# Solve stage of a hybrid token mixer: chunk masks and exponentials ahead of the low-rank decays, block and solution buffers in pairs

## The chip, the cores and the metric

The kernel runs on one core of one Trainium2 chip. The metric is the device time of one execution in microseconds; three executions of the kernel before are given, and one more was profiled.

## The reference

One layer of a bidirectional mixer over 1024 latent tokens and 256 context tokens, width 1024, all float32. The projected tokens feed two head groups. The first is gated DeltaNet (four heads, key and value width 128), computed in chunks. What the kernel calls the solve belongs to it:

```
diff = gc[..., :, None] - gc[..., None, :]
decay = where(incl, exp(where(incl, diff, 0)), 0)
lower = where(strict, einsum("nbhcd,nbhsd->nbhcs", kb, k) * decay, 0)
sol = triangular_solve(eye + lower, rhs, lower=True, unit_diagonal=True)
attn = einsum("nbhcd,nbhsd->nbhcs", q, k) * decay
```

The second is gated linear attention (GLA: four heads, key width 64, value width 128). It needs its own projections of q, k and v, and a decay per channel from a low-rank product:

```
gk = log_sigmoid(einsum("blzr,zrc->zblc", lr, w_gk) + b_gk) / 16
```

Both scan forward and backward. An output projection, a gated residual and a convolutional feed-forward network follow.

## The kernel before

The program is a sequence of blocks. In a block each of five engines (PE for matmuls, ACT for activations, DVE for vector work, POOL for vector work and memsets, SP for issuing DMAs) walks through its own list, written out by hand; semaphores order them, and the engines meet at a block's end. The change lies in the second block, the **solve stage** (lines 753 to 1167 in the trace). The first block makes the normalised inputs `hT`, the DeltaNet q, k, v and the product `lrab`; the block behind it scans the DeltaNet chunks.

The tokens are ten chunks of 128, taken in the order of `ORDER`; index m below is the place in that order, and d is the direction, forward or backward. The stage does three kinds of work side by side.

**The units** are GLA projections on PE, evacuated by ACT from three PSUM banks in turn (`unit`, L833 to L857 on PE; `evac`, L931 to L953 on ACT). A unit is 512 tokens wide, or 256 for the third part of a tile. `V0` to `V3` are value tiles (L851), `Q0`, `Q1`, `K0`, `K1` query and key tiles (L855), and `D0` to `D3` the low-rank decay products (L843, only 32 rows deep). The list `UNITS` numbers them; unit n waits for the evacuation of unit n-3 (L839). After a tile's last evacuation ACT issues the load of the weights two tiles on into `ws` (L953).

**The chunks**: `keys(m)` on PE makes the products k k and, for latent chunks (m from 2), k q (L871, L877). SP loads the cumulated decays of a chunk as rows broadcast to all partitions into `GR`, three buffers in turn (`g_rows`, L769), a buffer's next load waiting until the chunk that used it is done. POOL adds the mask (`mask`, L1044), ACT takes eight exponentials (`decays_of`, L977), DVE multiplies the products by them into `Wm` and `Am` (`chunk`, L1088 and L1094), SP stores those (`store`, L775 and L779).

**The solves**: three batches of 4, 4 and 2 chunks. SP reads 32x32 diagonal blocks of the stored `Wm` back into `blk` (`feed`, L787). DVE scales them into `co` (L1100, L1102) and runs 31 pairs of steps (`solve`, L1109 and L1112), each pair waiting for the one before. The result is in `so`, cleared by POOL before (`clear`, L1036), transposed by POOL into `st` after (`turned`, L1050), and stored by SP (`solutions`, L793 to L797). There is one `blk` and one `so`, so the next batch's `clear` waits until the stores of the batch before have landed.

**Low-rank decays**: `decay(j)` on ACT takes Abs, Exp and Ln of the 1280 columns of a D tile (L965 to L969), `decay(j)` on DVE one elementwise pass and a scan over them (L1076, L1079). They have one scratch tile `ga`.

At the start the gate tables are made by ACT and DVE in turn (L982 to L992, L1117 to L1146) with two small groups of PE products between (L889, L895), and end in the tile `rows`, from which SP stores what `g_rows` reads. At the end PE sums the modulation (`mg`, 32 products of one column each, L926), and DVE adds it up (L1164, L1166).

```
solve(0)
for m in range(6, NT):
    chunk(m)
solve(1)
solve(2)
```

Of the kernel before, what the change touches and what calls it, by code (L numbers as in the profile page):

```python
# [22 lines left out]
H = 4  # L23
# [62 lines left out]
def program(nc, x, c, ctx, c_ctx, w_mod, b_mod, norm1, w_in, gdn_conv, gdn_a_log, gdn_dt_bias, gdn_norm,  # L86
# [9 lines left out]
    with es:  # L96
# [113 lines left out]
        wlr = place("wlr", [P, KT, 48], 83)  # L210
        s_lw = sem("w_lrab_in")
# [22 lines left out]
        with nc.Block() as block:  # L234
            @block.sync
            def _(sp):
# [53 lines left out]
                rest(15)  # L290
                sp.wait_ge(s_ma, 64)
# [4 lines left out]
                sp.wait_ge(s_lw, 32)  # L296

# [399 lines left out]
        ws = [place(f"ws{i}", [P, KT, P], 142.25 + 4 * i) for i in range(2)]  # L697
# [5 lines left out]
        blk = place("blk", [P, BLK, BLK], 184)  # L703
        co = place("co", [P, BLK, BLK], 180)
        so = place("so", [P, BLK, BLK], 176)
# [16 lines left out]
        s_gr, s_grm, s_pm = [two(f"g_rows_in{u}") for u in range(3)], two("g_rows_masked"), two("decays")  # L722
# [8 lines left out]
        mg = [place(f"mg{i}", [P, 2, 512], (150.25, 159.25, 142.25, 146.25)[i]) for i in range(4)]  # L731
# [3 lines left out]
        for name in ("D0", "V0.0", "D1", "V0.1", "V0.2", "D2", "D3", "V1", "V2", "V3", "Q0", "Q1", "K0", "K1"):  # L735
# [17 lines left out]
        with nc.Block() as block:  # L753
            @block.sync
            def _(sp):
                def weights(n):
                    sp.dma_start(ws[n % 2][:, :, :], win[:, :, WCOL[n]:WCOL[n] + P]).then_inc(s_w3[n % 2], 16)

# [22 lines left out]
                def feed(b):  # L781
# [3 lines left out]
                    if b:  # L785
                        sp.wait_ge(s_sv, STEPS_S * b)
                    sp.dma_start(blk[0:32 * n, :, :], blocks_of(w_img, 2 * m0, 2 * n)).then_inc(s_fd[b], 16)  # L787

                def solutions(b):
# [3 lines left out]
                    sp.dma_start(blocks_of(x_img, 2 * m0, n), so[f, :, :]).then_inc(s_xw[b], 16)  # L793
                    sp.dma_start(blocks_of(xt_img, 2 * m0 + n, n), so[k, :, :]).then_inc(s_xw[b], 16)
# [4 lines left out]
                weights(0)  # L799
                sp.dma_start(v_dram.rearrange("c p n -> p c n"), vtok[:, :, :]).then_inc(s_vs, 16)  # L800
                weights(1)
# [13 lines left out]
                for m in range(4, 6):  # L815
                    store(m)
                    g_rows(m + 3)
                solutions(0)
                for m in range(6, 8):
# [14 lines left out]
            def _(pe):  # L834
                def unit(n):
# [21 lines left out]
                    mm.then_inc(s_um, 1)  # L857
# [26 lines left out]
                tile("D0")  # L884
                unit(UNIT[("V", 0, 0)])
# [6 lines left out]
                tile("D1")  # L892
# [34 lines left out]
                mm.then_inc(s_mq, 1)  # L927

# [1580 lines left out]
```

## Time and profile before

| | us |
|---|---|
| median of three runs | 1782.11 |
| lowest and highest | 1780.32, 1782.6 |
| profiled execution, its own time | 1779.76 |
| its span in the trace | 1777.7 |
| solve stage, first to first instruction of the next block | 298.4 to 505.2 |
| ACT's part of the gate tables, first Abs to the end of the sigmoid | 304.6 to 309.9 |
| PE's last product in the stage ends | 488.6 |
| DVE's last solve step ends | 498.9 |

The mean granted clock of PE is 0.956 over the span, where 1.00 is 2.4 GHz and 0.50 is 1.2 GHz. In a timeline each line is a run of like instructions of one engine: when the run starts, how long it takes, and in brackets how long the engine sat idle before it and who released it. The matmul counts of the trace are twice those of the program for float32.

### The profile page before, as it was taken

What the parts mean: (1) busy time and instruction counts of PE and PEld (TensorE: products, weight loads), DVE (VectorE), ACT (ScalarE), POOL (GpSimd) and SP (SyncE); (2) the same over time, 40 slices, a digit from 0 to 9 for tenths busy, and PEclk for the clock granted to TensorE, in tenths of its full rate; (3) what the DMA queues carried; (4) which work ended last, traced back from release to release, by engine and by line L of the source; (5) the groups of instructions that cost most, each with busy time, mean ns of one, the idle gap of its engine ahead of it and who ended that gap; (6) DMA issues with size and microseconds to landing.
All of it is one profiled execution on the core that took longest, in us unless ns stands there. A gap on an engine that the chain in (4) does not pass through costs nothing.

```text
span 1777.7 us, 20877 instructions
## 1 busy us (share of the span) xinstructions
PE 1651.0 (93%) x8249; PEld 1229.4 (69%) x8249; DVE 1217.4 (68%) x1747; ACT 554.8 (31%) x890; POOL 461.1 (26%) x436
## 2 busy tenths in 40 slices
PE   7997999899949979999949989999999999999997
PEld 2544545696649965665537768888888888788786
DVE  2548876376656648888765639999999998633635
ACT  2623233561023332222243432222222222332322
POOL 4000000422013326566422343333333332300000
PEclk9998998899869988999969999999999999999999
DMA  9374454367369841000032321111111111532242
GB/s 335 97 266 130 142 179 153 98 178 190 65 189 274 231 127 60 12 25 24 15 122 89 107 71 49 48 48 48 48 48 48 48 48 48 201 95 95 90 148 83
DMA packets 202172, 194.23 MB, mean 109 GB/s; under 512 B 41045, under 2 KB 156063, under 8 KB 201948
## 3 DMA queue, kind: packets, MB, share of 16 engines
q1 hardware_dynamic: 194972, 187.40, 33.6%
q10 hardware_dynamic: 6816, 5.24, 1.0%
q8 instruction: 65, 1.06, 0.2%
q14 instruction: 31, 0.25, 0.1%
q0 software_dynamic: 288, 0.27, 0.0%
HBM read 150.77 MB, written 42.11 MB: 109 GB/s over the span
## 4 chain that ended last, share of the span: by engine, by line
PE 47%; DVE 7%; ACT 2%; DMA 2%; issue 2%; POOL 1%; SPq 0%; ACTq 0%; POOLq 0%
PE PS L2115 9%; PE PS L2117 9%; PE PS L2119 9%; PE PS L2152 4%; PE PS L2154 4%; PE PS L2156 4%; PE PS L1622 4%; PE PS L1635 2%; DVE Qbd L1833 2%; DMA ogb<-og_spill 2%; POOL xr L2312 1%; DVE AT L1849 1%; PE PS L1670 1%; DVE Ex L1814 1%; DVE oss L2344 0%
## 5 line engine op out<-in xcount | busy, mean ns | idle before, releaser
L2432 DVE SCALAR_TENSOR_TENSOR acc<-PS,fcol,acc 128x945 f32<-128x945 f32 (+2 forms) x176 | 215.2, 1222 | 35.4 <-ACT acc L2195 29.9
L2432 DVE SCALAR_TENSOR_TENSOR act<-PS,fcol,act 128x945 f32<-128x945 f32 (+2 forms) x176 | 215.1, 1222 | 21.6 <-ACT act L2195 16.2
L2115 PE MATMUL PS<-h2hi,whi 128*128 128x512 f32 x704 | 219.9, 390 | 0.0
L2117 PE MATMUL PS<-h2lo,whi 128*128 128x512 f32 x704 | 219.7, 389 | 0.0
L2119 PE MATMUL PS<-h2hi,wlo 128*128 128x512 f32 x704 | 219.5, 389 | 0.0
L384 PE MATMUL PS<-hT,wq 128*128 128x512 f32 (+1 forms) x432 | 163.1, 537 | 0.0
L2302 POOL TENSOR_TENSOR wlo<-wu,whi 128x1024 fp32r<-128x1024 f32 x44 | 106.5, 2421 | 216.7 <-ACT whi L2188 216.7
L2117 PEld LDWEIGHTS PS<-h2lo,whi 128*128 128x128 f32 x704 | 132.5, 188 | 27.5
L2119 PEld LDWEIGHTS PS<-h2hi,wlo 128*128 128x128 f32 x704 | 132.4, 188 | 27.5
L2115 PEld LDWEIGHTS PS<-h2hi,whi 128*128 128x128 f32 x704 | 132.5, 188 | 27.4
L2443 DVE TENSOR_TENSOR wrlo<-wr,wrhi 128x1024 fp32r<-128x1024 f32 x41 | 50.2, 1225 | 129.6 <-ACT wrhi L2258 129.6
L384 PEld LDWEIGHTS PS<-hT,wq 128*128 128x128 f32 x432 | 82.0, 190 | 80.0 <-issue 77.3
L1622 PE MATMUL PS<-hT,wz 128*128 128x512 f32 x256 | 119.0, 598 | 0.0
L2152 PE MATMUL PS<-wrhi,ahi 128*128 128x512 f32 x352 | 109.5, 393 | 5.1 <-DVE yb L2451 2.2
L2154 PE MATMUL PS<-wrlo,ahi 128*128 128x512 f32 x352 | 109.9, 393 | 0.0
L2156 PE MATMUL PS<-wrhi,alo 128*128 128x512 f32 x352 | 109.6, 393 | 0.0
L2258 ACT ACTIVATE wrhi<-wr 128x1024 fp32r<-128x1024 f32 x44 | 46.7, 1060 | 152.9 <-DMA wr<-in_w_down_dram 152.9
L2195 ACT ACTIVATE act<-PS,fcol 128x1024 f32<-128x1024 f32 x22 | 26.6, 1207 | 205.8 <-PE PS L2119 205.8
L2328 POOL TENSOR_TENSOR act<-act,acc 128x1024 f32<-128x1024 f32 x22 | 53.7, 2442 | 107.7 <-DVE act L2432 107.7
L2152 PEld LDWEIGHTS PS<-wrhi,ahi 128*128 128x128 f32 x352 | 66.5, 189 | 20.0 <-issue 2.6
L851 PEld LDWEIGHTS PS<-ws,hT 128*128 128x128 f32 x640 | 76.5, 202 | 2.0 <-ACT gP L937 2.0
L851 PE MATMUL PS<-ws,hT 128*128 128x128 f32 x640 | 77.2, 285 | 0.6 <-ACT gP L937 0.6
(278 smaller groups left out, 2877.6 us busy)
## 6 DMA issues: line engine op xcount, KB each, us to landing
wm<-in_w_mod_dram SPq DMA_DIRECT2D x24, 1024.0 KB, 8.0
wu<-in_w_up_dram SPq DMA_DIRECT2D x44, 512.0 KB, 3.8
wr<-in_w_down_dram SPq DMA_DIRECT2D x44, 512.0 KB, 3.4
wq<-in_w_in_dram SPq DMA_DIRECT2D x12, 512.0 KB, 7.7
gdn_x_image<-ztile SPq DMA_DIRECT2D x10, 516.0 KB, 6.6
gdn_xt_image<-ztile SPq DMA_DIRECT2D x10, 516.0 KB, 6.3
GR<-gdn_gc_rows SPq DMA_DIRECT2D x20, 256.0 KB, 4.7
gdn_w_image<-Wm SPq DMA_DIRECT2D x20, 256.0 KB, 4.4
```

What stands on the lines that cost most here:

```text
L384: mm = pe.matmul(PS[:, BANK[kind] + b, 0:n], wq[kind][:, k, :], hT[:, k, t0:t0 + n], start=(k == 0), stop=(k == KT - 1))
L851: mm = pe.matmul(PS[:, o, q * P:(q + 1) * P], hT[:, k, t0 + q * P:t0 + (q + 1) * P], ws[wt % 2][:, k, :], start=(k == 0), stop=(k == KT - 1))
L1622: mm = pe.matmul(PS[:, 3, :], ws4[n % 2][:, k, :], hT[:, k, half * 512:(half + 1) * 512], start=(k == 0), stop=(k == KT - 1))
L2115: pe.matmul(PS[:, b + half, :], whi[k][u][:, kk, :], h2hi[:, 4 * half:4 * half + 4, kk, :], start=(kk == 0), stop=False)
L2117: pe.matmul(PS[:, b + half, :], whi[k][u][:, kk, :], h2lo[:, 4 * half:4 * half + 4, kk, :], start=False, stop=False)
L2119: mm = pe.matmul(PS[:, b + half, :], wlo[k][u][:, kk, :], h2hi[:, 4 * half:4 * half + 4, kk, :], start=False, stop=(kk == KT - 1))
L2152: pe.matmul(PS[:, 2 * t + half, :], ahi[u][:, tok], wrhi[u][:, cols], start=(f == 0), stop=False)
L2154: pe.matmul(PS[:, 2 * t + half, :], ahi[u][:, tok], wrlo[u][:, cols], start=False, stop=False)
L2156: mm = pe.matmul(PS[:, 2 * t + half, :], alo[u][:, tok], wrhi[u][:, cols], start=False, stop=(f == FT - 1))
L2302: g.tensor_tensor(wlo[k][f % 2][:, :, :], wu[k][f % 2][:, :, :], whi[k][f % 2][:, :, :], ALU.subtract).then_inc(s_wl[k], 1)
L2328: g.tensor_tensor(act[f][:, :], act[f][:, :], acc[f % 2][:, :], ALU.mult).then_inc(s_6g, 1)
L2432: tp = v.scalar_tensor_tensor(out=t_[:, r0:r1, c0:c1], in0=up[:, r0 + dr:r1 + dr, c0 + dc:c1 + dc], scalar=tap_col(j, k, f), in1=t_[:, r0: ...
```

## The change

The mathematics is unchanged. What changes is the order of the lists of all engines in the solve stage, and some buffers.

- The first value tile's weights get a buffer `wg0` that the first block already fills, from SP, behind its last weight loads. In the solve stage V0 is PE's first unit. It is split: three quarters of its first unit, the gate products, the last quarter.
- `UNITS` starts with V0, V1.0 and V1.1; the tiles D0 and D1 come behind V1.1, D2 and D3 behind V1.2 and two keys.
- DVE masks chunks 0 to 3, POOL chunks 4 to 9.
- ACT takes the exponentials of chunks 0 to 7 before any D unit, and the four low-rank decays between V2 and Q1.
- DVE works through chunks 0 to 5, and in `solve` it does other work after 13 of the 31 pairs of steps: chunks 6 and 7 in batch 0, `decay(1)` in batch 1, `decay(3)` in batch 2.
- `blk` and `so` become two buffers each, used in turn. `so1` shares its place with the second half of `gq`, so the evacuation of Q1.0 waits for all stores of batch 1. `blk1` and `st` lie over `lrab`, so their first use waits for D3.
- The loads of `mg` are issued together by ACT, and PE's `mg` products come ahead of tile K1.

The diff, cut to its core:

```diff
@@ first block, SP @@
                 rest(15)
+                sp.wait_ge(s_qu, H)
+                sp.dma_start(wg0[:, :, :], win[:, :, GV0:GV0 + P]).then_inc(s_wg0, 16)
...
@@ solve stage @@
-        for name in ("D0", "V0.0", "D1", "V0.1", "V0.2", "D2", "D3", "V1", "V2", ...
+        for name in ("V0", "V1.0", "V1.1", "D0", "D1", "V1.2", "D2", "D3", "V2", ...
...
@@ SP @@
-                    if b:
-                        sp.wait_ge(s_sv, STEPS_S * b)
+                    if b == 1:
+                        sp.wait_ge(s_um, UNIT[("D", 3, 2)] + 1)
+                    if b == 2:
+                        sp.wait_ge(s_sv, STEPS_S)
...
                 feed(1)
+                solutions(0)
                 for m in range(8, NT):
                     store(m)
+                feed(2)
                 solutions(1)
-                feed(2)
                 solutions(2)
...
@@ ACT @@
+                        if (j, b) == (1, 0):
+                            a.wait_ge(s_xw[1], 64)
                         ev = a.activation(gq[:, j, t0:t0 + w], ...
...
@@ POOL @@
                 clear(0)
+                clear(1)
                 g.wait_ge(s_mn, 1)
-                for m in range(8):
+                for m in range(4, NT):
                     mask(m)
                 turned(0)
-                clear(1)
...
@@ DVE @@
+                        if j == 12:
+                            for op, m in between:
+                                op(m)
...
+                for m in range(3):
+                    mask(m)
+                for m in range(3):
+                    chunk(m)
+                mask(3)
+                for m in range(3, 6):
+                    chunk(m)
+                solve(0, ((chunk, 6), (chunk, 7)))
+                chunk(8)
+                chunk(9)
                 decay(0)
-                chunk(0)
...
+                solve(1, ((decay, 1),))
                 decay(2)
...
+                solve(2, ((decay, 3),))
```

How the instructions stand is shown at three places. In these rows `gvtok` is the evacuation of a V unit, `gP` that of a D unit, `GR` the exponentials of a chunk (one row for each direction), `ga` a low-rank decay.

ACT before, from the second low-rank decay (`decay(1)`) to the first unit of V1:

```order
L965 ACTIVATE ga<-gP 128x1280
L967 ACTIVATE ga<-ga 128x1280
L969 ACT_TABLE_LOAD
L969 ACTIVATE ga<-ga 128x1280
L937 ACTIVATE gP<-PS,vcol 128x512 x2
L937 ACTIVATE gP<-PS,vcol 128x256
L977 ACT_TABLE_LOAD
L977 ACTIVATE GR_1461<-GR_1461,ngc 128x128 x4
L977 ACTIVATE GR_1462<-GR_1462,ngc 128x128 x4
L937 ACTIVATE gP<-PS,vcol 128x512 x2
L937 ACTIVATE gP<-PS,vcol 128x256
L941 ACTIVATE gvtok<-PS 128x4x128
```

The exponentials of one chunk (chunk 1) stand between the D tiles, and a low-rank decay ahead of them.

ACT in the change, from the evacuation of V1.0 (first row) to that of V1.2:

```order
L943 ACTIVATE gvtok<-PS 128x4x128
L981 ACTIVATE GR_1466<-GR_1466,ngc 128x128 x4
L981 ACTIVATE GR_1467<-GR_1467,ngc 128x128 x4
L981 ACTIVATE GR_1462<-GR_1462,ngc 128x128 x4
L981 ACTIVATE GR_1463<-GR_1463,ngc 128x128 x4
L981 ACTIVATE GR_1464<-GR_1464,ngc 128x128 x4
L981 ACTIVATE GR_1465<-GR_1465,ngc 128x128 x4
L943 ACTIVATE gvtok<-PS 128x4x128
L939 ACTIVATE gP<-PS,vcol 128x512 x2
L939 ACTIVATE gP<-PS,vcol 128x256
L939 ACTIVATE gP<-PS,vcol 128x512 x2
L939 ACTIVATE gP<-PS,vcol 128x256
```

The exponentials of chunks 5, 6 and 7 now stand between the evacuations of V1.0 and V1.1, and the D units behind them, with no low-rank decay near.

PE before, at the end of the stage (K0, K1, then the `mg` products):

```order
L855 MATMUL PS<-hT,ws_1456 128x512 x16
L855 MATMUL PS<-hT,ws_1456 128x256 x8
L855 MATMUL PS<-hT,ws_1457 128x512 x16
L855 MATMUL PS<-hT,ws_1457 128x256 x8
L926 MATMUL PS<-ones,mg_1482 128x1 x8
L926 MATMUL PS<-ones,mg_1483 128x1 x8
L926 MATMUL PS<-ones,mg_1484 128x1 x8
L926 MATMUL PS<-ones,mg_1485 128x1 x8
```

The one-column products close PE's list.

PE in the change, same place (K0, the `mg` products, K1):

```order
L856 MATMUL PS<-hT,wg_106 128x512 x16
L856 MATMUL PS<-hT,wg_106 128x256 x8
L927 MATMUL PS<-ones,mg_1487 128x1 x8
L927 MATMUL PS<-ones,mg_1488 128x1 x8
L927 MATMUL PS<-ones,mg_1489 128x1 x8
L927 MATMUL PS<-ones,mg_1490 128x1 x8
L856 MATMUL PS<-hT,ws_1460 128x512 x16
L856 MATMUL PS<-hT,ws_1460 128x256 x8
```

The one-column products moved ahead of the 24 products of tile K1.

DVE in the change, inside the first solve, after 13 pairs of steps:

```order
L1119 TENSOR_TENSOR blk_1479<-co,so_1482 128x19x13
L1122 TENSOR_TENSOR so_1482<-so_1482,blk_1479 128x19x13
L1092 TENSOR_TENSOR Wm_1468<-PS,GR_1462 128x512
L1092 TENSOR_TENSOR Wm_1469<-PS,GR_1463 128x512
L1098 TENSOR_TENSOR Am_1472<-PS,GR_1462 128x512
L1098 TENSOR_TENSOR Am_1473<-PS,GR_1463 128x512
L1092 TENSOR_TENSOR Wm_1470<-PS,GR_1464 128x512
L1092 TENSOR_TENSOR Wm_1471<-PS,GR_1465 128x512
L1098 TENSOR_TENSOR Am_1474<-PS,GR_1464 128x512
L1098 TENSOR_TENSOR Am_1475<-PS,GR_1465 128x512
L1119 TENSOR_TENSOR blk_1479<-co,so_1482 128x18x14
L1122 TENSOR_TENSOR so_1482<-so_1482,blk_1479 128x18x14
```

Chunks 6 and 7 stand there between two steps; before, they followed the solve's last step.

## Rows read from the trace of the kernel before

**Rows 1.** The page: busy time of the engines, share of the span, instructions.

```profile
PE 1651.0 (93%) x8249; PEld 1229.4 (69%) x8249; DVE 1217.4 (68%) x1747; ACT 554.8 (31%) x890; POOL 461.1 (26%) x436
```

**Rows 2.** PE, timeline of the stage: start us, us, engine line op out<-in xcount.

```profile
299.56 4.63 PE L843 MATMUL PS<-lrab,wgk 32*128 32x512 f32 x6
304.12 9.67 PE L851 MATMUL PS<-ws,hT 128*128 128x128 f32 x64
...
314.54 2.41 PE L843 MATMUL PS<-lrab,wgk 32*128 32x512 f32 x6
...
318.93 10.88 PE L851 MATMUL PS<-ws,hT 128*128 128x128 f32 x96
329.74 2.41 PE L843 MATMUL PS<-lrab,wgk 32*128 32x512 f32 x6
339.73 4.63 PE L843 MATMUL PS<-lrab,wgk 32*128 32x512 f32 x6 [7.58 <-ACT gP L937]
345.00 9.71 PE L851 MATMUL PS<-ws,hT 128*128 128x128 f32 x64 [0.65 <-ACT gP L937]
354.55 1.06 PE L871 MATMUL PS<-kT 128*128 128x128 f32 x8
...
358.12 10.88 PE L851 MATMUL PS<-ws,hT 128*128 128x128 f32 x96
...
422.16 55.14 PE L855 MATMUL PS<-hT,ws 128*128 128x512 f32 x144
477.14 11.44 PE L926 MATMUL PS<-ones,mg 128*128 128x1 f32 x64
```

**Rows 3.** Windows: busy us of PE, PEld, DVE, ACT, POOL, then granted clock, DMA, GB/s.

```profile
332.00:333.00 1.00, 0.15 (x1) 0.00 (x0) 0.01 (x1) 1.00 (x5) 1.00 (x1) 0.89 1.09 330
...
345.00:350.00 5.00, 5.00 (x24) 5.00 (x25) 0.60 (x2) 0.89 (x2) 0.49 (x1) 0.51 0.62 199
```

**Rows 4.** DVE, timeline of the stage.

```profile
317.34 0.42 DVE L1141 COPY rows<-PS 80x256 f32<-80x256 f32 x1 [2.13 <-PE PS L896]
...
344.35 1.26 DVE L1088 TENSOR_TENSOR Wm<-PS,GR 128x512 f32<-128x512 f32 x2
...
361.95 2.82 DVE L1079 TENSOR_TENSOR_SCAN gP<-cmask,gP 128x1280 f32<-128x1280 bf16 x1
...
434.32 1.22 DVE L1100 TENSOR_TENSOR co<-blk,nb 64x1024 f32<-64x1024 f32 x1 [2.46 <-DMA blk<-gdn_w_image]
...
447.04 0.42 DVE L1109 TENSOR_TENSOR blk<-co,so 128x252 f32<-128x252 f32 x1
...
460.79 0.19 DVE L1112 TENSOR_TENSOR so<-so,blk 128x31 f32<-128x31 f32 x1
472.73 1.21 DVE L1100 TENSOR_TENSOR co<-blk,nb 32x1024 f32<-32x1024 f32 x1 [11.75 <-DMA blk<-gdn_w_image]
```

**Rows 5.** POOL, timeline of the stage.

```profile
323.11 11.27 POOL L1044 TENSOR_TENSOR GR<-GR,mneg 128x512 f32<-128x512 f32 x6 [23.50 <-DMA GR<-gdn_gc_rows]
...
350.24 2.50 POOL L1044 TENSOR_TENSOR GR<-GR,mneg 128x512 f32<-128x512 f32 x2 [4.75 <-DMA GR<-gdn_gc_rows]
...
387.67 2.56 POOL L1044 TENSOR_TENSOR GR<-GR,mneg 128x512 f32<-128x512 f32 x2 [7.26 <-DMA GR<-gdn_gc_rows]
...
470.96 0.95 POOL L1036 MEMSET so<- 128x1024 f32 x1 [7.05 <-DMA gdn_x_image<-st]
```

**Rows 6.** SP, timeline of the stage.

```profile
374.88 0.37 SPq L787 DMA_DIRECT2D blk<-gdn_w_image  x1
...
382.84 1.63 SPq L769 DMA_DIRECT2D GR<-gdn_gc_rows  x2
```

**Rows 7.** ACT, timeline of the first block's end and of the stage.

```profile
296.53 0.38 ACT L531 ACTIVATE lrab<-PS 48x256 f32<-48x256 f32 x1 [4.24 <-PE PS L444]
...
388.98 2.56 ACT L977 ACTIVATE GR<-GR,ngc 128x128 f32<-128x128 f32 x8 [1.47 <-POOL GR L1044]
...
477.34 0.38 ACT L949 ACTIVATE gk<-PS 128x256 f32<-128x256 f32 x1 [2.86 <-PE PS L855]
```

More of the change, by code:

```diff
@@ L210, in program @@
         wlr = place("wlr", [P, KT, 48], 83)
+        wg0 = place("wg0", [P, KT, P], 142.25)
+        s_wg0 = sem("first_gla_value_weights_in")
         s_lw = sem("w_lrab_in")
@@ L296, in _ @@
                 sp.wait_ge(s_lw, 32)
+                sp.wait_ge(s_wg0, 16)
             @block.gpsimd
@@ L696, in program @@
         gq = place("gq", [P, 2, LAT], 197)
-        ws = [place(f"ws{i}", [P, KT, P], 142.25 + 4 * i) for i in range(2)]
+        ws = [wg0, place("ws1", [P, KT, P], 146.25)]
         ga = place("ga", [P, TOK], 150.25)
@@ L702, in program @@
         nb = [place(f"nb{b}", [P, BLK], 175.25 + 0.125 * b) for b in range(3)]
-        blk = place("blk", [P, BLK, BLK], 184)
+        blk = [place(f"blk{i}", [P, BLK, BLK], (192, 184)[i]) for i in range(2)]
         co = place("co", [P, BLK, BLK], 180)
-        so = place("so", [P, BLK, BLK], 176)
+        so = [place(f"so{i}", [P, BLK, BLK], (176, 201)[i]) for i in range(2)]
         st = place("st", [P, BLK, BLK], 188)
@@ L721, in program @@
         s_rd, s_nb = sem("rows_stored"), [sem(f"beta_blocks_in{b}") for b in range(3)]
-        s_gr, s_grm, s_pm = [two(f"g_rows_in{u}") for u in range(3)], two("g_rows_masked"), two("decays")
+        s_gr, s_grm, s_pm = [two(f"g_rows_in{u}") for u in range(3)], two("g_rows_masked_by_dve"), two("decays")
+        s_grp = two("g_rows_masked_by_pool")
         s_mn = sem("mask_ready")
@@ L814, in _ @@
                 feed(0)
[L815 to L819, printed above, removed]
+                for m in range(4, 8):
                     store(m)
@@ L883, in _ @@
                 tr.then_inc(s_lt, 1)
-                tile("D0")
-                unit(UNIT[("V", 0, 0)])
+                unit(UNIT[("V", 0, 0)], 0, 3)
                 pe.wait_ge(s_gd, 3)
@@ L891, in _ @@
                 mm.then_inc(s_gm, 1)
-                tile("D1")
+                unit(UNIT[("V", 0, 0)], 3, 4)
                 pe.wait_ge(s_gd, 4)
@@ L927, in _ @@
                 mm.then_inc(s_mq, 1)
+                tile("K1")
             @block.scalar
@@ new lines, in _ @@
+                decays_of(2)
+                evac(UNIT[("V", 0, 2)])
+                decays_of(3)
+                decays_of(4)
+                evac(UNIT[("V", 1, 0)])
+                decays_of(5)
+                decays_of(6)
+                decays_of(7)
+                evac(UNIT[("V", 1, 1)])
+                tile("D0")
+                tile("D1")
+                evac(UNIT[("V", 1, 2)])
+                decays_of(8)
+                tile("D2")
+                tile("D3")
+                decays_of(9)
@@ L1094, in chunk, with mask, solve @@
                             v.tensor_tensor(Am[u][d][:, :], PS[:, 6 + u, :], GR[m % 3][d][:, :], ALU.mult).then_inc(s_a[d], 1)
-                def solve(b):
+                def mask(m):
+                    for d in range(2):
+                        v.wait_ge(s_gr[m % 3][d], 16 * (m // 3) + 16)
+                        v.tensor_tensor(heads(GR[m % 3][d][:, :]), heads(GR[m % 3][d][:, :]),
+                                        mneg[:, d, :].unsqueeze(1).to_broadcast([P, H, P]), ALU.add).then_inc(s_grm[d], 1)
+                def solve(b, between):
                     n = 16 * BATCHES[b][1]
```

147 lines of the change are left out of this document (59 added, 88 removed).

## The prediction

> **What bounds the kernel now.** I read the page first: PE is busy for 93% of the span and DVE for 68% [rows 1], so time is to be had where PE waits. The front table then shows such a place: PE's last product of the solve stage ends at 488.6, the next block starts at 505.2, and between them stands DVE, whose last solve step ends at 498.9. The timelines say what each engine does there. On PE [rows 2] see three things: a gap of 7.58 us before D3, blocks of V products that take 9.7 us instead of 7.25, and no work after 488.6. On DVE [rows 4] see that batch 2 starts only at 472.73, after 11.75 us of idling for its blocks, because `so`, `blk` and SP's queue are shared. So before, the chain of solves sets the stage's end, with PE 16.6 us ahead of it. From 298.5 to 505.2 the stage takes 206.7 us. I ask how long each of the two engines needs in the new order; the later one sets the end.
>
> **DVE in the new order.** The changes there go together: second buffers, decays moved behind, 8 of 20 masks added. First the start. V0.0 takes D0's place, so the tile `rows` is copied when PE has done the transposes of `lrab` (1.1 us, from 298.5 to 299.56), V0.0 (9.7), the gate products and two transposes (0.8 + 0.2): at 310.3, plus 0.4 for the copy, 310.7 instead of 317.8 [rows 2, 4]. ACT's gate chain takes 5.3 us and now starts at about 301, in time for that. The first mask moves by the same 7.1 us, from 323.1 [rows 5] to 316.0. The masks on DVE have no row; the nearest is the multiplication of the same size, 0.63 us each [rows 4]. I take that; even at POOL's 1.25 us [rows 5] eight of them would cost 5 us more of an engine that turns out to have 24 to spare. Chunks 0 to 2 then finish at about 321, 323 and 325. From a finished chunk to the next mask on its buffer 4.6 us pass (345.6 to 350.24) [rows 4, 5], then 1.3 for two masks, 2.5 for eight exponentials [rows 7], 2.5 for the chunk: chunk 3 is done at 332.
>
> Chunk 6, in the middle of batch 0, needs keys(6), which PE reaches at 367.5 (below). From there: chunks 6 and 7, 5.0; the other 18 pairs of steps, 13.9 (447.04 to 461.0) [rows 4]; chunks 8 and 9, 5.0; decay(0), 1.5 + 2.8 = 4.3 [rows 4]: 395.7. Batch 1 takes 26.7 (434.32 to 461.0) [rows 4] and decay(1) 4.3: 426.7. Decay(2), batch 2 (26.2, from 472.73 to 498.9) and decay(3) bring DVE to 461.5. The stores and the block's end took 6.3 us after the last step (498.9 to 505.2): 467.8. If PE were no bound, the stage would end 37 us earlier. It is one, and this is where the expected gain goes.
>
> **PE in the new order.** PE's work is the same, product for product. From 298.5 to 488.6 are 190.1 us. Of that, 7.58 + 0.65 = 8.2 is idle [rows 2]. The clock costs the rest that can go: D0 and D3 take 4.63 instead of 2.41, 4.4 in all, and V0.0 and V1.0 take 9.67 and 9.71 where 64 products at the full clock take 10.88 x 64/96 = 7.25, 4.9 in all [rows 2]; the window from 345 to 350 shows the granted clock at 0.51, 1.2 GHz, to its end [rows 3]. What is left is **172.6 us**, the `mg` products' 11.4 at their present, mostly half clock included. To this the new order adds, in order of time:
>
> - V0.0 opens at half clock, as now, **2.4**. D0 was only beside it.
> - A stall at the third unit of D0, **7.3**, and it is the new wait. That unit reuses the bank of V1.1 and waits for ACT's evacuation, and ACT must first take the exponentials of chunks 5, 6 and 7. PE is there after 1.1 + 9.7 + 0.8 + 2.0 (to 318.93) + 10.9 + 3.6 + 7.25 + 3.6 + 7.25 + 1.9 = 48.1 us, at 346.6, with 3.6 for the keys of two chunks (354.55 to 358.12) [rows 2]. ACT: the rows of chunk 7 are loaded by SP behind `feed(0)`, which waits for chunk 3's stores, about 4.6 after 332, so 336.6. From that feed to the mask of the row tile queued behind it 12.8 us pass today (374.88 to 387.67) [rows 5, 6]: 349.4. Masks and exponentials end 3.9 after the mask's start (387.67 to 391.5) [rows 5, 7], the evacuation takes 0.6: 353.9. Lower bound: only SP's issues of four stores (2) and the load's own 4.8 (382.84 to 387.67) count, giving 347.9 and a stall of 1.3. Upper: every round of chunks a microsecond later, 11. I take the row that has the same feed in front.
> - After that stall the clock has fallen, as it had 0.7 us after D2 (window 332 to 333 at 0.89, then 0.50) [rows 2, 3]. The last D0 unit and D1 pay 2.22 x 1.2 = **2.7**, the V and key products behind them **2.4** like V1.0.
> - D2 and D3 in a row, 4.8 us of products 32 rows deep. D1 alone, between full products, kept the clock (2.41), but D2 with 0.7 us of idling lost it, and D3 at half clock did not bring it back: it rose only 4.9 us into V1.0 [rows 2, 3]. Between nothing and 1.8 + 2.4 = 4.2, I take half, **2.1**.
> - K1 behind the one-column products, which run at half clock (11.44 us for 64) [rows 2]: **2.4** again. Before, nothing followed them.
>
> A page speaks on the fourth item. The Trainium skill, TensorE: Matmul & The Clock Gate, Part 1, has the gate follow how busy PE is ("activity releases the throttle") and names no row count. By that, D2 and D3 would keep the clock, and the sum would be 2.1 lower; D3's row, busy from start to end and still at half clock, speaks against it.
>
> Sum: 172.6 + 2.4 + 7.3 + 2.7 + 2.4 + 2.1 + 2.4 = 191.9; PE ends at 490.4. The last evacuation takes 0.4 [rows 7]. Between the first block's last evacuation (296.9) and the next block 1.5 us passed [rows 7], semaphore clearing included, which is missing here; I take 0.7, between 0.2 and 1.5. The stage ends at **491.5 instead of 505.2: 13.7 us less**.
>
> **Edits costed at nothing.** The load of `wg0` stands in the first block behind SP's last weight load and lands while PE still has q, k, v and `lrab` products to do; without that cover V0.0 would start later by a load's 4 us or so. Batch 1's wait for D3 lies under chunks 8 and 9. The `mg` loads go out after V3, some 40 us before PE needs them. The evacuation of Q1.0 waits for batch 1's stores: DVE 426.7 plus 10.0 (460.98 to 470.96) [rows 4, 5] is 436.7. PE has that product at 490.4 - 19.6 - 11.4 - 17.2 - 6.9 = 435.3 (an eighth of 55.14 is a unit, 6.9 [rows 2]) and needs the bank only two units later, at 449.1. So 12.4 us cover it.
>
> The next block begins with loads from DRAM as before; I expect nothing there. In the profiled execution the time goes from 1779.76 to 1766.1. The median lies 2.35 above that execution, so I forecast 1782.1 - 13.7 = **1768.4** for a median.
>
> **Rivals.**
> 1. *PE is released early*: the loads behind `feed(0)` come without queueing, the stall is 1.3 and the D tiles keep the clock. 172.6 + 2.4 + 2.4 + 1.3 = 178.7, 13.2 below my sum: 1755.2. For it: D1's row. Against: 7.26 us of POOL waiting for row tiles even now [rows 5]. Chance 0.15; half ways to it lie in my range.
> 2. *Chunks run late*: keys(2) needs the first chunk's `Wm`, and PE gets there at 323.0, one or two us after it. If the first six row loads and masks take 5 us more, PE waits there 3.5 and at D0 3.5 more: 1775.4. For it: POOL's six masks took 11.27 instead of 7.5 [rows 5]. Chance 0.17.
> 3. *Slower*: the store of batch 1 comes so late that Q1.0's bank is not free. Every us beyond 12.4 is paid by PE; from 12.4 + 13.7 = 26.1 us on the kernel is no faster than before, and at 35 it takes 1782.1 + 8.9 = 1791. DVE would need a wait of that length ahead of batch 1, for instance decay(0) waiting for ACT behind V2.0. ACT has that at about 389, DVE asks at 391. Chance 0.03.
> 4. *The solves still bound the stage*: the moved work in the middle of each batch brings waits of 20 us, DVE and PE end together or DVE ends last, near 498: 1775 to 1782. Chance 0.05.
>
> **How the numbers follow.** My case, 1763 to 1773, has 0.60. The range 1758 to 1777 takes in rival 2 and part of 1 and 4. Both bounds of the stall (6.0 down, 3.7 up) with the clock's 2.1 either way give 8 down and 6 up around 1768.4, which the range holds. What a measurement here can tell from no change is 0.2%, 3.6 us. Rivals 1 and 2 and my case are all faster: 0.94 with most of rival 4; same 0.03, slower 0.03.
>
> **What would show it.** PE's last product of the stage is one of K1, ends near 490, and DVE has by then been done for over 20 us. PE has one idle gap of 5 to 10 us in D0, ended by the evacuation of V1.1, behind ACT waiting for POOL's mask of chunk 7. K1 takes about 19.6 us, V0.0's 64 products about 9.7. Wrong would be: DVE or SP last in the stage; a wait of ACT at Q1.0 that PE feels; a first block that ends later than 298.4; or a gap at keys(2).

## The result and the profile after

The changed kernel takes **1762.43 us** (median of four runs, 1760.85 to 1766.8); the kernel before took 1782.36 beside it (four runs, 1780.32 to 1782.66). The ratio on record is 0.9905, with a 95% interval of 0.9885 to 0.9925: faster by 0.95%. The quotient of the two medians alone is 0.9888; the kernel before had medians of 1780.2 to 1780.3 in the later series below, so a gain of 17 to 20 us is what the runs bear out. The forecast was 1768.4 with a range of 1758 to 1777. The profiled execution took 1761.43 us, 18.3 less than the 1779.76 of the profiled execution before; its span in the trace is 1759.5.

The page of the changed kernel, first part, answers to [rows 1]:

```profile
PE 1645.4 (94%) x8249; PEld 1224.1 (70%) x8249; DVE 1223.1 (70%) x1755; ACT 555.5 (32%) x890; POOL 441.9 (25%) x428
```

The instructions of PE are the same in number; it is busy for 5.6 us less in all, so most of the gain is time in which it stood. DVE has eight instructions more (the masks) and POOL eight fewer.

PE's timeline of the stage after the change, against [rows 2] (`...` stands for lines left out):

```profile
299.53 0.80 PE L884 MATMUL PS<-ident,lrab 48*128 48x48 f32 x10 [1.98 <-PEq L107]
300.25 7.20 PE L852 MATMUL PS<-wg,hT 128*128 128x128 f32 x48
...
308.11 2.03 PE L852 MATMUL PS<-wg,hT 128*128 128x128 f32 x16
...
344.26 1.98 PE L844 MATMUL PS<-lrab,wgk 32*128 32x512 f32 x4
354.85 5.48 PE L844 MATMUL PS<-lrab,wgk 32*128 32x256 f32 x8 [8.61 <-ACT gvtok L943]
360.26 6.10 PE L852 MATMUL PS<-ws,hT 128*128 128x128 f32 x32
...
369.87 4.56 PE L844 MATMUL PS<-lrab,wgk 32*128 32x512 f32 x12
374.35 7.41 PE L852 MATMUL PS<-wg,hT 128*128 128x128 f32 x64
...
458.42 8.54 PE L927 MATMUL PS<-ones,mg 128*128 128x1 f32 x64
466.82 19.43 PE L856 MATMUL PS<-hT,ws 128*128 128x512 f32 x48
486.97 1.06 PE L1339 MATMUL PS<-ident,kT 128*128 128x128 f32 x8 [0.72 <-PEq L759]
```

PE works to the very end: its last K1 product ends at 486.25 and the next block follows 0.7 us later, where before 16.6 us lay between. One stall is left, the 8.61 us at the third unit of D0, and it is the one that was forecast, with the releaser that was forecast: the evacuation of V1.1.

DVE's timeline after, against [rows 4]: a wait for keys(6), the start of batches 1 and 2, the end of the last solve.

```profile
367.29 1.29 DVE L1092 TENSOR_TENSOR Wm<-PS,GR 128x512 f32<-128x512 f32 x2 [5.99 <-PE PS L873]
...
396.89 1.19 DVE L1110 TENSOR_TENSOR co<-blk,nb 64x1024 f32<-64x1024 f32 x1
...
434.43 1.19 DVE L1110 TENSOR_TENSOR co<-blk,nb 32x1024 f32<-32x1024 f32 x1
...
464.44 0.18 DVE L1122 TENSOR_TENSOR so<-so,blk 64x31 f32<-64x31 f32 x1
```

The idle times in front of `co` (2.46 and 11.75 us before) are gone, and DVE is done with the solves at 464.6 instead of 498.9, 22 us ahead of the stage's end. The two engines have changed places. The stage takes 187.4 us from PE's first product to that of the next block (299.53 to 486.97), where it took 206.7. The rest of the program is as before: 1272.6 us from the stage's end to the end of the span (486.93 to 1759.5), and 1272.5 before (505.2 to 1777.7).

The wait behind the solves does come, as the prediction had it: ACT waits for batch 1's stores ahead of Q1.0, and PE does not feel it. ACT's timeline after:

```profile
437.84 0.60 ACT L948 ACTIVATE gq<-PS 128x512 f32<-128x512 f32 x1 [2.21 <-DMA gdn_x_image<-st]
```

### The profile page after: what moved, and what is told of

Read it like the earlier page. It is cut to its first block, busy times and chain, and to the rows that moved or that the text cites. A ratio compares the mean times of both kernels' runs of the same rounds, so it can differ in the third digit from the quotient of the medians.

```text
span 1759.5 us, 20882 instructions
## 1 busy us (share of the span) xinstructions
PE 1645.4 (94%) x8249; PEld 1224.1 (70%) x8249; DVE 1223.1 (70%) x1755; ACT 555.5 (32%) x890; POOL 441.9 (25%) x428
## 3 DMA queue, kind: packets, MB, share of 16 engines
q8 instruction: 65, 1.06, 0.2%
## 4 chain that ended last, share of the span: by engine, by line
PE 47%; DVE 7%; ACT 3%; DMA 2%; issue 2%; POOL 1%; SPq 0%; ACTq 0%; POOLq 0%
PE PS L2130 9%; PE PS L2128 9%; PE PS L2132 9%; PE PS L2165 4%; PE PS L2167 4%; PE PS L2169 4%; PE PS L1635 4%; PE PS L1648 2%; DVE Qbd L1846 2%; DMA ogb<-og_spill 2%; POOL xr L2325 1%; DVE AT L1862 1%; PE PS L1683 1%; DVE Ex L1827 1%; DVE oss L2357 0%
## 5 line engine op out<-in xcount | busy, mean ns | idle before, releaser
L1635 PEld LDWEIGHTS PS<-hT,wz 128*128 128x128 f32 x256 | 47.9, 192 | 42.4 <-issue 40.6
L2167 PEld LDWEIGHTS PS<-wrlo,ahi 128*128 128x128 f32 x352 | 67.1, 190 | 14.1
```

The source lines that it names most:

```text
L1635: mm = pe.matmul(PS[:, 3, :], ws4[n % 2][:, k, :], hT[:, k, half * 512:(half + 1) * 512], start=(k == 0), stop=(k == KT - 1))
L2167: pe.matmul(PS[:, 2 * t + half, :], ahi[u][:, tok], wrlo[u][:, cols], start=False, stop=False)
```

## The experiments

The experiments were timed in three series, each beside the kernel before on the same chip, whose median there was 1780.2 to 1780.3 us; the ratios are those on record. The diffs are condensed: words in brackets and lists with semicolons stand for several lines. "Stage" is the time from PE's first product in the solve stage to its first in the next block.

| kernel | median us | ratio, 95% interval | stage us | longest stall of PE in the D tiles |
|---|---|---|---|---|
| before | 1782.4 | 1 | 206.7 | 7.58 |
| changed | 1762.43 | 0.9905 (0.9885 to 0.9925) | 187.4 | 8.61 |
| e1_evac_first | 1753.11 | 0.9851 (0.9832 to 0.9869) | 180.2 | none |
| e2_mg_last | 1760.64 | 0.9892 (0.9873 to 0.9911) | 188.0 | 8.06 |
| e3_one_buffer | 1761.67 | 0.9898 (0.9877 to 0.992) | 190.3 | 7.79 |
| e4_load_late | 1768.97 | 0.9942 (0.9921 to 0.9962) | 193.4 | 7.73 |
| e5_sums_spread | 1747.57 | 0.9815 (0.9795 to 0.9835) | 175.3 | none |
| e6_tiles_spread | 1749.24 | 0.9828 (0.9808 to 0.9848) | 174.6 | 1.95 |
| e7_pool_masks | 1761.74 | 0.9898 (0.9877 to 0.9919) | 188.8 | 6.74 |
| e8_decays_late | 1790.58 | 1.0058 (1.0035 to 1.0081) | 215.6 | 1.26 |
| e9_tiles_apart | 1747.28 | 0.9818 (0.9796 to 0.984) | 171.9 | 0.82 |
| e10_decays_early | 1773.49 | 0.9961 (0.9948 to 0.9974) | 197.9 | 7.27 |

### The stall

```diff
@@ ACT, on the changed kernel @@
-                decays_of(7)
                 evac(UNIT[("V", 1, 1)])
                 tile("D0")
                 tile("D1")
+                decays_of(7)
                 evac(UNIT[("V", 1, 2)])
```

> ACT takes V1.1's evacuation and the evacuations of D0 and D1 ahead of the exponentials of chunk 7; nothing else is moved. Theory A (PE sets the end, and the wait at the third D0 unit plus the half clock behind it are lost time): the gap of 8.6 us goes, D1 and V1.2 run at full clock (5.1 us), PE's list ends 13 us earlier, near 473, where SP's last stores of batch 2 (about 471) are nearly level. About 1749 us, 1746 to 1753. Theory B (the wait only moves: V1.2's evacuation now stands behind chunk 7, and PE waits for it at D2): 4 to 6 us less, about 1757. Theory C (DVE sets the end): no change, 1762.

Measured: 1753.11, 9.3 us below the changed kernel, 0.1 above the range of theory A and 4 below the 1757 of theory B. PE's timeline shows why:

```profile
344.25 5.28 PE L844 MATMUL PS<-lrab,wgk 32*128 32x512 f32 x12
349.46 6.36 PE L852 MATMUL PS<-ws,hT 128*128 128x128 f32 x32
...
359.32 4.56 PE L844 MATMUL PS<-lrab,wgk 32*128 32x512 f32 x12
363.81 7.41 PE L852 MATMUL PS<-wg,hT 128*128 128x128 f32 x64
...
447.88 11.39 PE L927 MATMUL PS<-ones,mg 128*128 128x1 f32 x64
459.12 19.85 PE L856 MATMUL PS<-hT,ws 128*128 128x512 f32 x48
```

The whole stall is gone, so its cause is settled: ACT's wait for chunk 7's mask ahead of an evacuation that was ready. That PE's time comes off the kernel's also shows that PE sets the stage's end. The clock, which theory A gave back as well, is won back only in part. D0 and D1 still pay 0.7 us (5.28 against the 4.56 of D2 and D3) and V1.2 still takes 6.36 instead of 3.6. The `mg` products paid 2.9 us more than in the changed kernel, which the edit does not touch. The stage adds up: 187.4 - 8.6 for the stall - 2.2 in D0 and D1 + 2.9 + 0.7 in V1.2 and K1 = 180.2, as in the trace.

### The one-column products

```diff
@@ PE, on the changed kernel @@
-                (the 32 mg products)
                 tile("K1")
+                (the 32 mg products)
```

> PE's one-column products go back behind tile K1. Theory A (the clock): K1 takes 17.2 instead of 19.4 us, but DVE's last two instructions (3.0 us) then follow PE's end, and the products themselves take between 8.5 (as in the changed kernel) and 11.4 us (as before). Together 0 to 3 us more: 1763 to 1766. Theory B (the place of these products is free either way): within 1 us of 1762.4.

Measured: 1760.64, within the noise of the changed kernel. K1 takes 17.35 us again (19.43 behind the sums), and the sums take 11.63 instead of 8.54, a difference that comes with both places (see below). Something behind the sums pays in either order: here the next block opens at half clock (its first eight products take 1.94 us instead of 1.06). That is 0.9 us against the 2.1 of K1, so their place may be worth about 1 us, which these runs cannot tell from nothing. The larger loss is the run of thin products itself, so the next edit breaks it up:

```diff
@@ PE, on the kernel of e1 @@
+                def sums(i):
+                    (the 8 products of mg[i])
-                tile("K0")
-                (the 32 mg products)
-                tile("K1")
+                unit K0.0; sums(0); unit K0.1; sums(1); unit K0.2
+                unit K1.0; sums(2); unit K1.1; sums(3); unit K1.2
```

> On top of e1_evac_first (1753.1 us), PE's 32 one-column products are no longer one run: eight each stand behind the first and second unit of K0 and of K1. Theory A (a run of them loses the clock, and the K units behind it pay): all stay at full clock, the 64 records take about 7.4 us instead of 11.4 and K1 17.2 instead of 19.9, so 4 to 7 us less than e1: 1746 to 1749. Theory B (the products are slow by themselves, the clock is not the cause): within 1.5 us of e1.

Measured: 1747.57, 5.5 us below e1, as theory A had it. PE's timeline of e5 and the windows around the first two groups (busy us of PE, PEld, DVE, ACT, POOL, granted clock, DMA, GB/s):

```profile
433.61 7.03 PE L856 MATMUL PS<-hT,wg 128*128 128x512 f32 x16
440.47 1.84 PE L926 MATMUL PS<-ones,mg 128*128 128x1 f32 x16
442.18 7.11 PE L856 MATMUL PS<-hT,wg 128*128 128x512 f32 x16
449.13 1.84 PE L926 MATMUL PS<-ones,mg 128*128 128x1 f32 x16
```

```profile
440.00:443.00 3.00, 3.00 (x20) 2.36 (x19) 2.86 (x6) 0.60 (x1) 0.00 (x0) 1.00 0.02 5
443.00:449.00 6.00, 6.00 (x15) 2.66 (x14) 5.76 (x9) 0.00 (x0) 0.00 (x0) 1.00 0.00 0
```

Four groups take 7.4 us instead of 8.5 to 11.6, nothing behind them pays, and the clock is at 1.00 in both windows. The experiment changes the place of the sums and the length of the run together, but e2 showed that the place alone gives no 5 us.

### Which parts of the change carry the gain

The second buffers:

```diff
@@ on the changed kernel @@
-        blk = two places, so = two places
+        blk = [place("blk", [P, BLK, BLK], 192)] * 2
+        so = [place("so", [P, BLK, BLK], 176)] * 2
@@ SP @@
-                feed(1); solutions(0); stores; feed(2); solutions(1)
+                solutions(0); feed(1); stores; solutions(1); feed(2)
@@ ACT, ahead of Q1.0 @@
-                            a.wait_ge(s_xw[1], 64)
```

> The changed kernel with one block buffer and one solution buffer, and the waits of the kernel before for them; the order of all engines stays, but SP's feeds stand behind the stores of the batch before again. Theory A (PE sets the end and DVE has some 15 us to spare): DVE's last step is 7 to 12 us later, the time stays, 1761 to 1764. Theory B (the second buffers carry the gain): 1770 or more.

Measured: 1761.67, the same. DVE does wait for its blocks again and ends later, just under the 7 to 12 us that were expected, but inside the reserve. DVE's timeline of e3:

```profile
440.99 1.21 DVE L1106 TENSOR_TENSOR co<-blk,nb 32x1024 f32<-32x1024 f32 x1 [4.20 <-DMA blk<-gdn_w_image]
...
471.12 0.18 DVE L1173 TENSOR_TENSOR mods<-PS,vcol 128x32 f32<-128x32 f32 x1
471.33 2.82 DVE L1175 SCALAR_TENSOR_TENSOR gain<-mods,vcol 128x8 f32<-128x8 f32 x1
```

The last step ends at 471.2, 6.6 us later than in the changed kernel and still 18 us ahead of the stage's end. Of the 2.8 us that this trace's stage is longer, 2.7 are the `mg` products (11.27 against 8.54), which the edit does not touch.

The masks on DVE:

```diff
@@ on the changed kernel @@
 POOL
-                for m in range(4, NT):
+                for m in range(NT):
                     mask(m)
 DVE
-                for m in range(3):
-                    mask(m)
...
-                mask(3)
```

> The changed kernel (1762.4 us) with all masks on POOL again, as in the kernel before; orders and buffers stay. Theory A (chunks come in turn with the row loads, POOL's 1.25 us a mask against DVE's 0.65 shows only at the first six): chunk 0 to 3 are 2 to 4 us later, the wait in D0 grows by as much: 1763 to 1767. Theory B (DVE relieved of eight masks is worth something): 1758 to 1761, PE unchanged and DVE earlier.

Measured: 1761.74, the same. POOL does its first six masks in 7.4 us (it took 11.27 before, [rows 5]), and DVE's first chunk starts at 319.37 instead of 321.29, since the masks of chunks 0 to 2 no longer stand ahead of it on DVE. Theory A missed the mechanism: chunks 0 to 3 come no later, and the wait in D0 does not grow but is 6.74 us, where the five other traces that have it show 7.27 to 8.61. Theory B had DVE right, which is earlier, but not the time. The stage is 188.8 us all the same. The `mg` products take 2.4 more (10.94), V2.0 1.5 more (8.94) and K1 0.9 more (20.32), all of it clock. Moving masks to DVE therefore won nothing; whether it cost the 0.5 to 1.9 us of the longer wait, these runs cannot tell.

The early load of the first weights:

```diff
@@ SP, on the changed kernel @@
 first block
-                sp.wait_ge(s_qu, H)
-                sp.dma_start(wg0[:, :, :], win[:, :, GV0:GV0 + P]).then_inc(s_wg0, 16)
 solve stage
+                sp.dma_start(ws[0][:, :, :], win[:, :, WCOL[0]:WCOL[0] + P]).then_inc(s_w3[0], 16)
                 sp.dma_start(v_dram.rearrange("c p n -> p c n"), vtok[:, :, :]).then_inc(s_vs, 16)
```

> The first value tile's weights are loaded at the start of the solve stage instead of in the first block. Theory A (the cover counts): PE's first V product waits for the load, about 7 to 8 us, the gate products stand behind it, so everything moves: 1769 to 1771. Theory B (PE's later wait in D0 absorbs it): 1762 to 1765.

Measured: 1768.97, 6.5 us above the changed kernel: near theory A, though the wait itself is 3.2 us and not 7 to 8. PE's timeline of e4:

```profile
302.19 0.79 PE L881 MATMUL PS<-ident,lrab 48*128 48x48 f32 x10 [1.99 <-PEq L107]
306.16 8.24 PE L849 MATMUL PS<-wg,hT 128*128 128x128 f32 x48 [3.18 <-DMA wg<-in_w_in_dram]
```

The stage is 6.0 us longer. The wait for the load is 3.2 of it, V0.0 at a lower clock 1.0 (8.24 against 7.20), V2.0 1.6 (9.04 against 7.41) and the `mg` products 2.1 (10.68 against 8.54); the stall, V1.2 and K1 give back 2.1. The first two, 4.2, are the edit's; how much of the clock further on belongs to it one trace doesn't tell. The load that the first block covers is between a fifth and a third of the change's gain, 4.2 to 6.5 of 19.9 us.

The low-rank decays late, in the old order and early in the new one:

```diff
@@ e8, on the kernel before: ACT @@
-                decay(0) ... decay(3) among the chunks 0 to 3
+                decay(0), decay(1) around Q0.1; decay(2) behind K0; decay(3) behind K1, then mg[0]'s load
@@ e8: DVE @@
                 solve(0); chunks 6 to 9
+                decay(0); decay(1)
                 solve(1)
+                decay(2); decay(3)
                 solve(2)
```

> The kernel before with one part alone: the low-rank decays of ACT and DVE stand behind the chunks, as in the change (decays 0 and 1 ahead of the second solve, 2 and 3 ahead of the third); buffers, units, masks and first weights stay, and the mg load that shares ga's place goes last. Theory A (alone it brings nothing, since PE's place for the keys and the late stores decide when chunks 8 and 9 and the solves run, and the decays then stand before a solve): the first solve starts some 12 to 16 us earlier, the second no earlier, and the stage ends 5 to 12 us later: 1787 to 1794. Theory B (this move carries the gain): 1762 to 1772.

```diff
@@ e10, on the changed kernel: ACT @@
                 tile("D1")
+                decay(0)
                 evac(UNIT[("V", 1, 2)])
+                decay(1)
                 decays_of(8)
                 tile("D2")
                 tile("D3")
+                decay(2)
...
@@ e10: DVE @@
-                solve(0, ((chunk, 6), (chunk, 7)))
+                solve(0, ((decay, 0), (decay, 1), (chunk, 6), (chunk, 7)))
```

> This is the changed kernel with the four low-rank decays early again: on ACT decay(0) and decay(1) behind D1, decay(2) and decay(3) behind D3; on DVE decay(0) and decay(1) ahead of chunk 6 in the first solve, decay(2) and decay(3) ahead of the second. Masks, pairs of buffers and PE's order stay. With the kernel before, e8 (old order, decays late, 1790.6) and the changed kernel (1762.4) it makes a square of two by two. Theory A, PE sets the end and DVE has some 20 us to spare, so that the decays' place costs only what PE feels: ACT evacuates the first D2 unit behind decay(1) and chunk 8, some 5 us later than now, so PE stands 3 to 6 us at D3: 1765 to 1769, and DVE's last solve step still ends between 460 and 470. Theory B, the decays behind the chunks are what makes the solves end in time: DVE is last again, and the time goes back to 1775 or more.

Measured: e8 1790.58, e10 1773.49. DVE's timeline of e8 at the start of batch 2, and PE's of e10 at D2 and D3:

```profile
477.69 1.49 DVE L1076 SCALAR_TENSOR_TENSOR gP<-gP,ga 128x1280 f32<-128x1280 f32 x1 [10.34 <-ACT ga L969]
...
481.96 1.19 DVE L1100 TENSOR_TENSOR co<-blk,nb 32x1024 f32<-32x1024 f32 x1
```

```profile
368.19 2.41 PE L844 MATMUL PS<-lrab,wgk 32*128 32x512 f32 x6
376.15 4.63 PE L844 MATMUL PS<-lrab,wgk 32*128 32x512 f32 x6 [5.55 <-ACT gP L939]
380.71 9.15 PE L852 MATMUL PS<-wg,hT 128*128 128x128 f32 x64
```

In e8 DVE sets the end. Batch 2 starts 9.2 us later (481.96 against 472.73 in [rows 4]), and the stage ends 9.1 later. The line of DVE above names the reason: it waits 10.34 us for ACT's last low-rank decay, and that one stands behind the evacuations of K1. ACT's timeline of e8:

```profile
471.23 1.27 ACT L965 ACTIVATE ga<-gP 128x1280 f32<-128x1280 f32 x1
```

PE waits too in e8, 15.18 us for the last load of `mg`, but its sums are done 14.6 us before the next block. In this form late decays alone make the kernel **slower** by 0.6%. The first solve did start 14.2 us earlier and the second no earlier (433.89 against 434.32), as theory A said. But ACT's last two decays stand later here than in the change, where all four come ahead of Q1. Decay(2) is through on DVE at 467.4 and a decay takes 4.3 there. With ACT's last decay ready, batch 2 would by estimate have started near 472, as in the kernel before: then the late decays bring nothing in the old order, and cost nothing either. That kernel was not run.

In e10 the end belongs to PE and DVE's last solve step is at 467.7, as theory A said, but the price was misjudged: 1773.49 lies between the two theories. The stage is 10.5 us longer than in the changed kernel: 5.55 for the stall at D3, 2.2 for D3 at half clock, 1.7 for V2.0 and 2.2 for the `mg` products (10.72), less 1.3 at the first stall; what V1.2 pays, K1 gives back. The profiled execution was the lowest of eight.

In the square of two by two, moving the decays late costs 10.3 us in the old order and wins 11.1 in the new one (10 by the ratios). The corners are not quite the same edit, since ACT's decays have other places in each. What the traces show is narrower than a rule: a decay costs what the engine behind it has to wait, DVE's last solve in e8 and PE's D3 in e10.

### Where the D tiles stand

```diff
@@ e6, on e5: PE; ACT evacuates D0 behind chunk 5, D1 behind V1.1 @@
-                V1.0, keys 4 5, V1.1, D0, D1, V1.2, keys 6 7, D2, D3, V2.0
+                V1.0, keys 4 5, D0, V1.1, D1, V1.2, keys 6, D2, keys 7, D3, V2.0
@@ e9, on e5: PE; ACT's evacuations follow @@
-                V1.0, keys 4 5, V1.1, D0, D1, V1.2, keys 6 7, D2, D3, V2.0
+                V1.0, keys 4 5, V1.1, D0, V1.2, keys 6, D1, keys 7, D2, V2.0, D3
```

> On top of e5_sums_spread, the D tiles are spread: D0 behind V1.0 and keys, D1 behind V1.1, D2 between the keys of chunks 6 and 7, D3 behind them. Theory A (two D tiles in a row can lose the clock): no D tile is over 2.5 us, V1.2 takes 3.6, and 1 to 4 us less than e5, about 1745. Theory B (DVE and SP are the bound by now): no change against e5.

> This is the kernel of e5 with the four D tiles each alone between full products: D0 behind V1.1, D1 behind keys(6), D2 behind keys(7), D3 behind V2.0; on ACT each evacuation of a D tile behind the unit before it. In e5 PE's D0 and D1 take 5.77 us instead of 4.8, V1.2 6.01 instead of 3.6 and V2.0 9.04 instead of 7.3, 5 us for the clock; in e6 the same spreading won 3.4 of it but paid 1.95 for a stall and 1.6 for the clock behind that. Theory A, the clock falls in a run of two D tiles and not in one: no stall here, since D0 stands behind V1.1 again, and 2 to 5 us less than e5: 1743 to 1746. Theory B, the chip takes the clock away once per stage wherever the first short break or the first thin products come: the loss only changes its place, 1746 to 1750.

Measured: 1749.24 and 1747.28, both the same as e5 within the noise. Neither median is in theory A's range; that of e9 is in theory B's. The traces show more than the medians, of one execution each. PE's timeline of e5, then of e6, then of e9:

```profile
345.40 5.77 PE L844 MATMUL PS<-lrab,wgk 32*128 32x512 f32 x12
351.10 6.01 PE L852 MATMUL PS<-ws,hT 128*128 128x128 f32 x32
...
360.61 4.56 PE L844 MATMUL PS<-lrab,wgk 32*128 32x512 f32 x12
365.10 9.04 PE L852 MATMUL PS<-wg,hT 128*128 128x128 f32 x64
```

```profile
337.70 2.41 PE L844 MATMUL PS<-lrab,wgk 32*128 32x512 f32 x6
342.06 8.91 PE L852 MATMUL PS<-ws,hT 128*128 128x128 f32 x64 [1.95 <-ACT gP L948]
```

```profile
343.33 2.41 PE L844 MATMUL PS<-lrab,wgk 32*128 32x512 f32 x6
345.68 3.84 PE L852 MATMUL PS<-ws,hT 128*128 128x128 f32 x32
...
358.78 7.41 PE L852 MATMUL PS<-wg,hT 128*128 128x128 f32 x64 [0.82 <-ACT gP L948]
366.12 2.41 PE L844 MATMUL PS<-lrab,wgk 32*128 32x512 f32 x6
```

In e5 a pair of D tiles costs clock both times. In e6 D0 stands so early that ACT is behind, PE waits 1.95 us, and V1.1 pays 1.6 for it. In e9 every D tile takes 2.41 and V1.2 and V2.0 run at full clock: the stage is 171.9 us, 3.4 less than in e5, and the profiled execution took 1742.82. That execution is the fastest of five; the other four took 1744.85 to 1754.74, and where they lose is open. So the gain of tiles that stand singly is shown in one trace and not in the median. e5 and e9 have the lowest medians of this study, 15 us below the changed kernel, with e6 2 us above them.

## Why the prediction was right, step by step

**What bounds.** Right. The solves no longer end last; PE does, with DVE 22 us ahead. The gain that was expected on DVE (37 us) was cut to PE's measure, as the prediction said.

**PE's sum.** 191.9 us were forecast from PE's first product to its last, and 186.7 were measured (299.53 to 486.25). Term by term:

| term | forecast | measured | from |
|---|---|---|---|
| V0.0 at half clock | 2.4 | 2.0 | 7.20 + 2.03 against 7.25 |
| stall in D0 | 7.3 | 8.6 | idle time at 354.85 |
| D0's third unit and D1 | 2.7 | 2.7 | 1.98 + 5.48 against 4.8 |
| what stands behind them | 2.4 | 2.5 | 6.10 against 3.6 |
| D2 and D3 | 2.1 | 0 | 4.56; V2.0 7.41 |
| `mg` products above 11.4 | 0 | -2.9 | 8.54 |
| K1 | 2.4 | 2.1 | 19.43 against 17.35 |

The terms account for 4.3 of the 5.2 us; the rest is spread over the other runs of products and was not followed up. **Two terms were mis-sized.** For D2 and D3 half of a range was taken, and in this execution the lower end came. The `mg` products were carried over "at their present, mostly half clock included", and that was no property of their place: by these windows the clock fell 2.4 us into the run before and 5.6 us into it after. Windows of the kernel before, then of the changed kernel (granted clock is the third number from the end):

```profile
477.00:480.00 3.00, 3.00 (x27) 2.97 (x25) 2.69 (x10) 0.38 (x1) 0.00 (x0) 0.93 0.47 126
480.00:483.00 3.00, 3.00 (x16) 3.00 (x15) 2.76 (x8) 0.00 (x0) 0.00 (x0) 0.50 0.12 49
```

```profile
461.00:464.00 3.00, 3.00 (x29) 3.00 (x28) 2.66 (x11) 0.00 (x0) 0.00 (x0) 1.00 0.00 0
464.00:467.00 3.00, 3.00 (x16) 3.00 (x16) 0.56 (x4) 0.00 (x0) 2.30 (x1) 0.50 0.53 87
```

In the eight traces that have this run in one piece with no idling in front (before, changed, e1 to e4, e7, e10) it took 8.54 in the changed kernel and 10.68 to 11.63 in the other seven. That run stands in the same place in e1, e3, e4, e7 and e10 as in the changed kernel, so the saving of 2.9 belongs to this one execution, not to the change. It was luck, and so was the lower end for D2 and D3: together they are 5.0 of the 5.6 us by which the stage's gain (19.3) passed the forecast (13.7). In e2, e3 and e7, whose medians are those of the changed kernel, the stage takes 188.0 to 190.3 us, a gain of 16 to 19.

**The stall.** Place, releaser and chain were right, by e1. The mask of chunk 7 came at 350.34 (forecast 349.4) and its exponentials ended at 354.3. PE was there at 346.2. ACT idled 6.11 us for it, in the timeline of ACT after:

```profile
351.76 2.56 ACT L981 ACTIVATE GR<-GR,ngc 128x128 f32<-128x128 f32 x8 [6.11 <-POOL GR L1046]
354.22 0.57 ACT L943 ACTIVATE gvtok<-PS 128x512 f32<-128x512 f32 x1
```

The prediction took ACT's order as given and did not see that another order, that of e1, is free of this wait.

**DVE's sum.** The first mask came at 316.14 (forecast 316.0), chunk 6 at 367.29 (367.5), batch 1 at 396.89 (395.7), batch 2 at 434.43 (431.0 by the sum), the last step at 464.6 (461.5). Batch 1 was 1.2 late, and one term was missing: the scan of decay(2) took 5.37 us instead of 2.82, beside POOL's transposition of batch 1.

**Edits costed at nothing.** The second buffers: right (e3). The masks have no effect on the time either (e7), though not at nothing: on DVE they stand ahead of chunk 0 and start it 1.9 us later than POOL's did. The cover of `wg0`'s load, "4 us or so" without it: right in kind, near in size. e4 shows 4.2 for the wait and V0.0's clock, 6.5 in the median.

**The stage's end.** 0.68 us from PE's last product to the next block's first instruction (486.25 to 486.93), where 1.1 was forecast.

**A first block that ends later** was named as something that would make the prediction wrong, and it came: PE's first product at 299.53 instead of 298.48. It is scatter, not the load of `wg0`: e2, e9 and e10 have that load too, and start at 298.55 to 298.76; e4 has none in that block and starts at 302.19. Net of it the stage gave 19.3 us and the run 18.3; the median, of four runs, gave 19.9.

The likeliest case held, and rival 1 was half true: the D tiles kept the clock in one place, and the stall was not short. The Trainium skill, TensorE: Matmul & The Clock Gate, Part 1, by which D2 and D3 would keep the clock, gave the better number for the profiled execution. The runs do not make it a rule: the same pair was followed by a slowed V2.0 in e4 and e5 (9.04) and in e7 (8.94). The same part of that page calls the number of slow products at a kernel's start run-variable. The traces show such variation in the middle of a kernel too, 8.54 to 11.63 us for one run of products.

## What to carry to other kernels

When a chain of waits on one engine sets a stage's end, add up the other engine's own time in the new order first: it caps the gain, and what lies below the cap (here the second buffers and the masks on DVE, each measured at nothing) need not be built. In an engine's hand-written list, an evacuation that is ready must not stand behind work that waits for a third engine; one line of ACT's list was worth 9 us. A long run of one-column products is better cut into small groups among full ones (5.5 us here); for products 32 rows deep the same is shown in one trace only. A part of a change is worth what waits behind it, and that differs between the old order and the new one, so try it on both sides and read in the trace who waits.

Not every part was taken alone. The early load, the buffers, the masks and the decays' place were; the new order of PE's units and keys, with the chunks' exponentials ahead of the D tiles, was not, and the parts' prices need not add up to the gain.

## What the runs showed of the hardware that was not expected

**The clock's fall is not fixed in the program.** The same 64 one-column products took between 8.54 and 11.63 us, depending on when the granted clock went from 1.00 to 0.50 (2.4 to 1.2 GHz) in them: by the windows of four traces 2.2 us into the run (11.63, e2), 2.4 (11.44, before), 3.2 (10.68, e4) and 5.6 (8.54, changed). A pair of D tiles was sometimes free and sometimes cost 1.6 us in V2.0 alone. Cut into groups of 16 records, the one-column products ran at full clock in e5, e6 and e9, and the D tiles that stood singly did in e6 and e9. What decides the moment is not shown.

**POOL slows DVE on small vector work, by far more than its size.** The last `gain` of DVE, eight columns, takes 0.17 us in e2, e5 and e10, where POOL is idle, and 2.81 in the kernel before, where POOL transposes `st` in the same time. POOL's and DVE's timelines of the kernel before, then DVE's of e2:

```profile
498.95 2.84 POOL L1050 TENSOR_TENSOR st<-so,ones 64x1024 f32<-64x1024 f32 x1 [26.83 <-DVE so L1112]
```

```profile
499.01 2.81 DVE L1166 SCALAR_TENSOR_TENSOR gain<-mods,vcol 128x8 f32<-128x8 f32 x1
```

```profile
486.05 0.17 DVE L1179 SCALAR_TENSOR_TENSOR gain<-mods,vcol 128x8 f32<-128x8 f32 x1
```

DVE's instruction starts 0.06 us behind POOL's and ends 0.03 us behind it, as if it stood until POOL was through. In e1 it starts at 459.53, in the middle of POOL's transposition (458.23 to 461.07), takes 1.57 us and ends at 461.10. In e10 half of `co` took 4.44 us beside POOL's transposition (439.18 to 442.96) and takes 1.88 without it (at 435.65 in the changed kernel). The Trainium skill, GPSIMD Engine Reference, section Key points, says that GpSimd shares SBUF interfaces with VectorE and contends with DVE instructions of two SBUF inputs; `gain` reads `mods` and `vcol`, and the rows agree. Before, 2.8 us of this lay between the last solve step and the end of DVE's work in the stage, beside SP's last stores; whether it cost the kernel before anything was not tried.
